# A gated MLP rewritten in the form of the two dense MLPs: seven block products for v, u and half of its second product

## The reference, cut to what matters

```python
def gmlp_spatial_gating(h, w_uv, v_gain, w_s, s_bias, w_o):
    uv = jax.nn.gelu(h @ w_uv, approximate=False)      # 1024x1024 @ 1024x4096
    u, v = jnp.split(uv, 2, axis=-1)                   # 2048 features each
    v = layer_norm(v, v_gain)
    s = jnp.einsum('gij,bnjgc->bnigc', masked w_s, v) + s_bias   # 128x128 mixes of tokens
    return (u * s) @ w_o                               # 1024x2048 @ 2048x1024

def squared_relu_mlp(h, w1, w2):                       # hidden width 4096
    return jnp.square(jax.nn.relu(h @ w1)) @ w2
...
    mod = (cond @ mod_w[i] + mod_b[i])                 # six parts of 1024 per layer
```

## Time and profile before

| | us |
|---|---|
| median of 3 runs (2212.44 to 2213.98) | 2213.45 |
| the profiled execution, its own time | 2209.18 |
| its span, first to last instruction | 2207.3 |
| PE busy, 97% of the span | 2147.6 |
| DVE busy, 65% | 1441.1 |
| POOL busy, 39% | 856.0 |
| ACT busy, 36% | 805.4 |
| gated MLP, from its opening (about 954) to the next one (about 1532) | 578 |

### The profile page before, as it was taken

The page is one execution under the profiler, slowest core; times in us unless marked ns, Lnnn a source line. Parts: engine busy times, 40 slices in busy tenths (PEclk is TensorE's granted clock), DMA queues, the critical chain, the costliest instruction groups (busy, mean ns, idle before and its releaser), DMA issues. The chain is left out here.

```text
span 2207.3 us, 27453 instructions
## 1 busy us (share of the span) xinstructions
PE 2147.6 (97%) x9916; PEld 1750.0 (79%) x9916; DVE 1441.1 (65%) x1749; ACT 805.4 (36%) x1141; POOL 856.0 (39%) x510
## 2 busy tenths in 40 slices
PE   6999999999999999999999999999999999999999
PEld 3886687788887888787888888888778888788887
DVE  8689689766657877565445531456776666776574
ACT  4337543343344442333222210223334334443341
POOL 0124413555556565301211222122155555564753
PEclk8999999999999999999999999999999999999999
DMA  7463532444465665224454221223234444654352
GB/s 271 121 181 93 216 98 80 148 158 153 158 221 184 216 209 177 90 86 166 159 189 143 95 75 52 72 76 96 67 138 157 154 153 156 220 188 161 102 183 90
DMA packets 154114, 317.26 MB, mean 144 GB/s; under 512 B 30225, under 2 KB 36241, under 8 KB 153490
## 3 DMA queue, kind: packets, MB, share of 16 engines
q1 hardware_dynamic: 107618, 199.49, 27.4%
q10 hardware_dynamic: 46384, 116.27, 14.8%
HBM read 238.12 MB, written 76.55 MB: 143 GB/s over the span
## 5 line engine op out<-in xcount | busy, mean ns | idle before, releaser
L641 POOL TENSOR_TENSOR w_lo<-w_raw,w_hi 128x1024 fp32r<-128x1024 f32 x80 | 198.0, 2476 | 818.5 <-ACT w_hi L765 818.5
L1909 PE MATMUL pp<-h_hi,w_hi 128*128 128x512 f32 x1056 | 364.3, 399 | 20.8 <-POOL w_lo L641 7.7
L2255 PE MATMUL pp<-hid_lo,w_hi 128*128 128x512 f32 x896 | 351.8, 393 | 11.6 <-POOL w_lo L714 6.9
L1909 PE MATMUL pp<-h_lo,w_hi 128*128 128x512 f32 x1056 | 355.9, 391 | 0.0
L1909 PE MATMUL pp<-h_hi,w_lo 128*128 128x512 f32 x1056 | 355.7, 391 | 0.0
L2255 PE MATMUL pp<-hid_hi,w_hi 128*128 128x512 f32 x896 | 349.6, 390 | 0.0
L2255 PE MATMUL pp<-hid_lo,w_lo 128*128 128x512 f32 x896 | 349.2, 390 | 0.0
L2255 PE MATMUL pp<-h_hi,w_hi 128*128 128x512 f32 x672 | 263.0, 391 | 8.0 <-DVE w_lo L1652 6.3
L996 ACT ACTIVATE w_hi<-mod_t 128x512 fp32r<-128x512 f32 x224 | 141.5, 632 | 336.2 <-POOL mod_t L709 174.6
L2255 PE MATMUL pp<-h_lo,w_hi 128*128 128x512 f32 x672 | 262.4, 391 | 0.0
L2255 PE MATMUL pp<-h_hi,w_lo 128*128 128x512 f32 x672 | 262.4, 391 | 0.0
(11 more groups left out here) (217 smaller groups left out, 3327.7 us busy)
## 6 DMA issues: line engine op xcount, KB each, us to landing
hid_dram<-wide_f SPq DMA_DIRECT2D x217, 256.0 KB, 2.9
w_raw<-weights SPq DMA_DIRECT2D x106, 512.0 KB, 3.5
wide_f<-hid_dram ACTq DMA_DIRECT2D x53, 1024.0 KB, 5.7
w_raw<-weights SPq DMA_DIRECT2D x168, 256.0 KB, 3.0
mod_t<-mod_w ACTq DMA_DIRECT2D x48, 512.0 KB, 4.9
wide_f<-weights SPq DMA_DIRECT2D x56, 256.0 KB, 4.3
mod_first<-mod_w SPq DMA_DIRECT2D x16, 512.0 KB, 15.4
mod_late<-mod_w ACTq DMA_DIRECT2D x2, 4096.0 KB, 22.8
```

The costliest lines, as they stand in the source:

```text
L641: nc.gpsimd.tensor_tensor(out=w_lo[:, s, :, :], in0=w_raw[:, s, :, :], in1=w_hi[:, s, :, :].bitcast(f32), op=ALU.subtract).then_inc(lo_don ...
L1909: last = T.matmul((pp[s] if tile is None else tile)[:, cs], w[:, s, k, :], r[:, k, cs], start=(k == 0 and w is w_hi and r is hi), stop=(k ...
L2255: last = T.matmul(bank, w[:, i, :], r[:, i, :], start=(t in FRESH and i == 0 and w is high and r is hi), stop=(i == QUADS - 1 and w is low ...
```

## The change

The gated MLP becomes a third object of `class Layer` between the two MLPs (`fast = [Layer(layer) for layer in range(3)]`, `gated` for the middle one). Its 16 pairs of v and u (8 of v, then 8 of u) run as the up pairs: 2 plain, 14 fast. v is turned after the products, 4 transposes at a time (`turn`), statistics over 256 columns at a time (`stats`), stored as half blocks. The 32 `mod` rows become 64 half rows of 512 in a ring of four loads (`load_row`, `use_row`); `V_ROWS` says how many DVE takes after which product. In the u pairs `blend`, `scale` and `gate` work on 512 columns; normalising v moves from DVE to ACT (`normalise`). Gated outputs go to `hid_dram` (for the first group of 4 pairs with differences, for the second only the 4 blocks); the second product is one fast group and one `closing`.

In all three: DVE makes the low parts of products 3 and 4 of the first pair before `plain_outputs(1)`; ACT makes `weight_high(0, 3)` before the last `rectify`; pairs that feed a closing store no differences. The norm of the gated MLP is scaled in `g_f` instead of `tmp`, without a wait.

```diff
-DOWN_GROUPS = (MLP_GROUPS - 1, MLP_GROUPS)
+DOWN_GROUPS = (MLP_GROUPS - 1, 1, MLP_GROUPS)
+FIRST_OUT = (0, VCH // 2, 0)
+V_FAST = VCH // 2 - PLAIN_PAIRS
+V_ROWS = ((0, 1, 1, 0, 2, 2, 3), (3, 2, 2, 0, 2, 2, 2), (2, 2, 2, 2, 2, 0, 0),
+          (2, 2, 1, 2, 2, 1, 1), (2, 2, 1, 0, 2, 2, 2), (2, 2, 2, 2, 2, 0, 0))
+COLUMNS_AFTER = ((1, 3), (2, 5), (4, 3), (5, 5))
+TURNS_AFTER = ((0, 5), (0, 6), (1, 1), (1, 2))
+BLENDS = ((4, 5, 7, 8), (3, 4, 6, 7)) + 6 * ((2, 3, 5, 6),)
...
+                def turn(k):
+                    j, turned = k // 4, k % 4
+                    pe.wait_ge(v_gelu, max(4 * j + 2 + turned // 2 * 2, 4))
+                    if k >= 2:
+                        pe.wait_ge(v_copied, k - 1)
+                    for b in range(2):
+                        for m in range(2):
...
+                            last = T.transpose(pp[3][:, at:at + P], v_block(j, 2 * (turned // 2) + m)[:, block:block + P], ident[:, :])
+                    last.then_inc(vtr_mm, 1)
...
+                    for part, after in enumerate(COLUMNS_AFTER):
+                        if L.gated and (n, t) == after:
+                            pe.wait_ge(v_gelu, 4 * n + 8)
+                            mod_columns(None, mt_used, RING_GV + 16 * part + 16, tile=pp[(n + 1) % 2])
...
+                def load_row(r):
+                    if r >= 4:
+                        act.wait_ge(mt_used, RING_GV + r - 3)
...
+                    act.dma_start(v_row[r % 4], mod_w[4 * KC + RING_GV + r // 2][:, columns_of(r % 2)]).then_inc(row_in[r % 4], 16)
...
+                def use_row(r):
+                    dve.wait_ge(row_in[r % 4], 16 * (r // 4) + 16)
...
+                    V.scalar_tensor_tensor(out=part, in0=v_row[r % 4], scalar=cond[:, 2, k:k + 1], in1=part,
+                                           op0=ALU.mult, op1=ALU.add).then_inc(mt_used, 1)
...
-                for t in (2, 4, 6):
+                operand_low(2)
+                if L.gated:
+                    stats(2)
+                    stats(3)
+                for t in (4, 6):
                     operand_low(t)
-                plain_outputs(1, (pp[1], pp[2]), (tmp[:, 0, :], mod_acc[:, :]))
+                weight_low(0, 3)
+                weight_low(0, 4)
+                if not L.gated:
+                    plain_outputs(1, (pp[1], pp[2]), (tmp[:, 0, :], mod_acc[:, :]))
```

More of the change, by code:

```diff
@@ L432, in output @@
             def output(self, j, o):
+                if self.gated:
+                    return stage(7 if j == UP_PAIRS - 1 and o == O_B11 else GATED[o])
                 if j == 0:
@@ L479, in load_block, with load_blocks @@
                 sp.dma_start(w_raw[:, s, :, :], weights[pair * 2 + (s + skip)]).then_inc(raw_in[s], 16)
+            def load_blocks(first, last, skip):
+                with sp.Fori(first, last) as pair:
+                    for s in range(2):
+                        load_block(pair, s, skip)
             def load_fast(L):
                 def load_quad(n, a):
-                    sp.dma_start(L.raw_quad(n, a), weights[L.pair_row(n, a // 2), :, QUADS * (a % 2):QUADS * (a % 2) + QUADS, :]).then_inc(L.quad_landed(n, a)[0], 16)
+                    row = weights[L.pair_row(n, a // 2)]
+                    quarter = row[:, QUADS * (a % 2):QUADS * (a % 2) + QUADS, :]
+                    if L.gated and n >= FAST_UP:
+                        quarter = row.rearrange("p (k two) f -> p two k f", two=2)[:, a % 2, :, :]
+                    sp.dma_start(L.raw_quad(n, a), quarter).then_inc(L.quad_landed(n, a)[0], 16)
                 def load_early(n):
@@ L1113, in fast_mlp @@
                         group_operand(L.group_of(n), t + 5)
-                    if last and t == 6:
+                    if last and t == 6 and not L.gated:
                         act.wait_ge(f_sum, L.threes + 3 * n + 3)
@@ L1937, in normed_pair, with closing @@
                 last.then_inc(gemm, 1)
-            def closing(pair0, hi, lo, n, chunk_ready=None, after=None, columns=None, first=None, begun=False, quads=None):
+            def closing(pair0, hi, lo, n, columns=None, begun=False, quads=None, order=None):
                 if not begun:
@@ L2222, in plain_unit @@
                         last = products(s, k, h_hi, h_lo, tile=tile)
+                        if k in (2, 5):
+                            for i in turns[k // 3:k // 3 + 1]:
+                                turn(i)
                     last.then_inc(gemm, 1)
@@ L2272, in _ @@
             fast_mlp(fast[0])
             pe.wait_ge(x_ev, fast[0].updates(fast[0].pairs - 1, 6))
-            closing(U_MLP[0] // 2 + PLAIN_PAIRS, h_hi, h_lo, 2, quads=fast[0].lows_ready(DOWN_GROUPS[0], 0))
-            def v_turn(c, s, pair):
-                pe.wait_ge(evac[s], pair + 1)
-                if not static(c) or c:
-                    pe.wait_ge(v_copied, c)
-                for b in range(KC):
-                    last = T.transpose(pp[2][:, P * b:P * b + P], tmp[:, s, P * b:P * b + P], ident[:, :])
-                last.then_inc(vtr_mm, 1)
@@ L2318, in _ @@
             fast_mlp(fast[1])
+            pe.wait_ge(x_ev, fast[1].updates(fast[1].pairs - 1, 6))
+            closing(fast[1].first + PLAIN_PAIRS, h_hi, h_lo, 3, quads=fast[1].lows_ready(DOWN_GROUPS[1], 0), order=GO_ORDER)
+            fast_mlp(fast[2])
 def kernel(x, c, positions, norm1_gain, norm2_gain, mod_w, mod_b, swa_w_qkv, swa_q_gain, swa_k_gain,
```

877 lines of the change are left out of this document (521 added, 356 removed).

## The result

| | before | changed | difference |
|---|---|---|---|
| median of 4 runs each, us | 2213.62 | 2189.62 (2188.55 to 2190.59) | -24.0 |
| profiled execution, us | 2209.18 | 2189.19 | -20.0 |
| its span, us | 2207.3 | 2187.4 | -19.9 |
| forecast median, us | | 2179 (2167 to 2195) | -34.5 |

The ratio is 0.9894, with a 95% interval of 0.988 to 0.9908. The change makes the kernel faster, by two thirds of what was forecast.

The account below looks back on a forecast made before the run. PE was taken as the bound, with no room in any stage. Matmuls at -49.0 and the other terms summed to -34.5 us: 2209.2 became 2174.7, plus 4.3 for the median 2179 us, range 2167 to 2195.

Parts of the forecast that it names:

- forecast case: Whole kernel: the median falls in 2172 to 2187 us, around the forecast 2179; chance 0.52.
- rival B: v stretch: DVE becomes the bound, every POOL operation stopping it, 22 in place of 8; 2193 to 2198; 0.24 with milder C.
- mild C: v stretch: milder form of the row-load ring turning too slowly for its landings; 2187 to 2207, chance 0.24 together with B.
- signs of being wrong: Fast v pair over 24 us; half rows at 0.75 without PE idle; or gated-stage idles long enough for the lower clock.
- term 1: Matmuls: 2304 before, 2088 after, 216 fewer at 0.2267 us each, -49.0 us.
- term 2: Interruptions of PE by transposes, blends and mod columns, four at a time: 32 more, +2.9 us.
- term 7: Other two MLPs: earlier low split shortens PE's waits for w_lo of product 3, -3.6 us.
- term 4: v stretch, six fast pairs: DVE asked for 20.8 of 21.4 us a pair, some at bad moments, +8 us.
- Gated opening: Opening of the gated stage: shorter h_lo waits, new waits for low weights and first product's weights, +0.6 us.
- upper bound of 22: v stretch: all seven POOL operations of a pair stop DVE for their 1.29 us, 6 x 3.6 = 22 us.
- u pairs: u pairs: DVE and ACT fit; square roots and ACT table changes delay ACT once, +1 us (0 to 4).
- Up to down, closing: Late operand split at the change to down products, +3.3 us; closing waits 2.28 + 0.89 instead of 0.90, +2.3 us.

Follow-up runs that it names:

- quarter rows: Changed kernel with each row load from the fifth on cut to a quarter of its bytes, DVE's 64 operations kept: 2178.25 us, ratio 0.985.
- The run with one input: Changed kernel with each half row computed as row x scalar, without adding the sum, so only one SBUF tensor is read: 2182.47 us, ratio 0.9857.
- six tiles: Changed kernel with the row sums kept in PSUM and the ring of row tiles made of six instead of four: 2172.85 us, ratio 0.9819.
- the PSUM sums with four tiles: Changed kernel with the row sums kept in idle PSUM halves and the clearing of mod_acc gone, ring still of four: 2180.3 us, ratio 0.9839.
- the low splits alone: Kernel before, with only the earlier low splits and weight_high(0, 3) ahead of the last rectify in the two MLPs; gated MLP plain: 2204.8 us, ratio 0.9967.
- the Gelu first: Changed kernel with ACT's Gelu of a block ahead of the weight_high of four products later in the v stretch: 2189.62 us, ratio 0.9888.

## Why the prediction was right, and where it was off

The direction and the range held, and so did the mechanism: PE's matmuls fall by 216, and what is lost again is idle time of PE in the v stretch. The size was 14.5 us too large in the trace (-34.5 against -20.0). The forecast case did not come; what came is rival B in its number and the mild C in its cause. Two of the prediction's own signs of being wrong appeared: fast v pairs of over 24 us, with DVE idle before rows for a DMA, and idles in the gated stage that were long enough for the lower clock. That the range held is owed to its upper part, which took in some of B. The gated stage, between the same two steps of its opening and of the next one, went from 577.9 to 563.7 us, -14.2, where terms 1 to 6 sum to -30.9.

| part | forecast | measured |
|---|---|---|
| matmuls, 216 fewer (term 1) | -49.0 | -49 |
| idle time of PE in the gated stage (terms 3 to 6) | +15.2 | +20.6 (3.1 to 23.7) |
| lower clock on its matmuls | 0 | +6.0 |
| interruptions and the rest (term 2) | +2.9 | about +8 |
| first and last part of the kernel (term 7) | -3.6 | -5.8 |

1. **Matmuls.** Right. Full-clock pieces of the v stretch still run at 0.23 us per matmul.
2. **Interruptions.** Too low by 5, of which 2.7 are the three `mod_columns` at the lower clock, the cost of term 4 over again. The other 2 to 3 I did not take apart.
3. **Gated opening.** Right: 0.40, 0.36 and 1.43 for the three waits left.
4. **The v stretch.** This is the step that failed, as a size. I put +8. The rows alone cost 19.4 (the run without them), close to my upper bound of 22, though by another route: that bound was POOL at its worst, rival B. *A row's time* was right: 0.67 and a share of the 4.3 for POOL make 0.96, and the average is 0.95 (0.75 alone, up to 1.78 beside POOL). *The landing* was not: "just in time at 3.0" put it at nothing. The 3.0 was the median of the whole kernel, and the loads of this stretch take 3.9 to 4.0, with 205 GB/s moving from 1045 to 1185 us in place of the 152 of an MLP's up pair. I had even forecast 230 there, and did not draw the conclusion. DVE stood 12.1 us waiting for rows, and without that landing the kernel is 11.8 us faster. With it gone, the rows cost 7.6 (2177.79 against 2170.21) or, as quarter rows, 8.0: what I had put for the whole term. That was the mild form of rival C, and I had given it no price of its own in the sum. The places were right: a Gelu before a turn, a row before `mod_columns`.
5. **u pairs.** 3.2 in place of 1 (1.93, 0.73 and 0.56), released by the normalisation on ACT; I had taken the low part of 0 to 4. Only the 1.93 is the delay by the square root that I had named: the other two stay when it moves, and what makes them is open.
6. **Up to down, closing.** 2.1 in place of 3.3; and 2.28 + 0.88 before the closing, as forecast (2.28 + 0.89, which is 2.3 more than the 0.90 of before).
7. **The other MLPs.** The last one waits 2.67, forecast 2.7, for the ACT copy named; the 2.7 of clock that I had left to the range came back. Alone on the kernel before this piece gave 7 to 8 us in the medians and 5.3 in the trace, of which 4.4 lie behind the opening of the last MLP. The 1.0 us that came in front of the gated opening holds the unsteady place of the first MLP, told below, and is no measure of this term.

**The clock** is where the sum had no term at all. I had written that no row shows it after idles of 2.28 and less, which was true of the trace before. In the trace after, waits of 1.63 and 1.87 with 0.7 us of work between them were enough at 1111.73, and the very same 2.28 before the first closing, followed by full clock in the trace before, is followed by 0.51 (in 10 of the study's 14 traces it is followed by the lower clock, in 4 not). With several idles of this size the safe term is that some of them cost 1.7 to 1.9 us more (half of a slow stretch of 3.4 to 3.8).

**The rule of the Trainium skill**, "SBUF — State Buffer", "Who interferes with whom", was cited against the change, and the runs bear it out where two inputs are concerned. With both in SBUF a row takes 0.75 us alone and up to 1.78 beside POOL (0.91 to 1.03 on average in the traces that have this operation), with the second one in PSUM 0.74 to 0.76 in either case. The run with one input is no third witness: its TENSOR_SCALAR takes 0.49 alone and up to 1.57 beside POOL. The rule's worst reading, all of POOL's operations in series with DVE's, is not what happened: taking the sums off the port, and the clearing with them, was worth 9 to 11 us of a possible 22.

## What to carry to other kernels

When a stage is filled up with small loads and small operations, price them by the stage's own traffic: a landing time of the whole kernel's median is too short for the stretch that moves the most, and a ring is deep enough only if its lead exceeds the landing under that load. An accumulator that is read and written for every row is the first thing to move to idle PSUM: its row then took 0.75 us beside GpSimd as without it, and the tiles that the ring lacked came free. Having one SBUF input was not enough for that here: look at an operation's longest time beside GpSimd, not at the mean of its group. And while DVE was late, another order on ACT only moved PE's wait (0.7 us longer in the stretch); with the rows' waits gone the same edit shortened the stretch by 1.4 us, and a part of PE's wait moved even then. Last, read an edit in the stretch where it acts: two of these traces differed by 2.9 us before they reached it.

## What the runs showed of the hardware that I had not expected

- **Landing under load.** A store of 256 KB of v landed in 4.1 us beside the rows' loads, in 2.4 beside loads of a quarter of their bytes, in 2.0 without them (205, 129 and 101 GB/s from 1045 to 1185 us). The traffic is not all of it: with the sums in PSUM they landed in 3.6 and 3.5 at 211 and 220 GB/s.
- **The lower clock is not a function of the idle alone.** PE's idle in the opening of the last MLP was 2.67 to 2.72 us in the changed kernel and in all eleven kernels made from it. The clock fell behind it in six of the twelve traces (those without rows and with six tiles among them), and in six it did not (the changed kernel, the PSUM sums with four tiles). After the 3.14 to 3.21 us near 361 us it fell in twelve of the study's fourteen traces and stayed at 1.00 in two (the low splits alone, the Gelu first), while in the changed kernel 1.93 was followed by 0.50.
- **Two outcomes at one place.** At the opening of the first MLP PE waits 0.5 or 2.3 us where the low splits come first, and 1.49 or 4.45 where they come last, in kernels that are alike up to there. In the short cases PE had waited 0.7 us for POOL's low weights near 392 us, in the long ones it had not. A difference between single traces at this place says nothing of an edit. What sets the outcome stays open.
